# Reordering VectorE and ScalarE work at the end of the branch stage and in the output stage of a two-layer trunk kernel

## The reference, cut to what matters

```
proj = jnp.einsum('btnw,nwd->btnd', branches, p['w_branch'])        # four branches, each 256 wide
gsig = jax.nn.sigmoid(gates...)                                      # one gate per branch and channel
merged = jnp.sum(gsig * proj, axis=2)
x = x + g1 * (merged @ p['w_out'])
h2 = _rms(x, p['g_norm2']) * (1 + sc2) + sh2                         # needs the sum of squares of all of x
x = x + g2 * _conv_ffn(h2, p['w_up'], p['conv_w'], p['conv_b'], p['w_down'])
```

## Time and profile before

| | before |
|---|---|
| median of 3 executions | 1292.45 us |
| lowest and highest | 1290.4 and 1293.11 us |
| the profiled execution's own time | 1288.97 us |
| its span | 1287.2 us |
| PE busy | 1266.9 us, 98% |
| DVE busy | 787.5 us, 61% |
| ACT busy | 594.0 us, 46% |
| POOL busy | 85.8 us, 7% |
| mean granted TensorE clock | 1.00 |

### The profile page before, as it was taken

How to read it: one execution, slowest core, us unless ns; L and a number is a source line. 1 busy time by engine, 2 the same in 40 slices (tenths; PEclk the granted TensorE clock), 3 DMA queues, 4 the chain that set the end, 5 groups by cost and what they waited for, 6 DMA issues and landing times.

```text
span 1287.2 us, 20265 instructions
## 1 busy us (share of the span) xinstructions
PE 1266.9 (98%) x8210; PEld 1184.3 (92%) x8210; DVE 787.5 (61%) x1482; ACT 594.0 (46%) x989; POOL 85.8 (7%) x57
## 2 busy tenths in 40 slices
PE   7999999999999999999999999999999999999999
PEld 6987888889989999999989888888898899999998
DVE  5553286448778777763353543864496787778432
ACT  3456455543355445442344564645433654454321
POOL 0000000005410000000000000000082000000000
PEclk9999999999999999999999999999999999999999
DMA  9731344543633444448554313344336233333343
GB/s 374 287 131 57 118 172 147 197 148 111 232 135 130 158 153 154 154 158 280 175 214 142 115 66 115 115 159 147 120 130 241 90 130 131 123 123 131 131 134 129
DMA packets 52686, 198.11 MB, mean 154 GB/s; under 512 B 6320, under 2 KB 6736, under 8 KB 51184
## 3 DMA queue, kind: packets, MB, share of 16 engines
q1 hardware_dynamic: 52272, 196.11, 43.4%
q0 software_dynamic: 320, 0.69, 0.2%
HBM read 194.51 MB, written 2.26 MB: 153 GB/s over the span
## 4 chain that ended last, share of the span: by engine, by line
PE 88%; DVE 7%; ACT 1%; issue 1%; DMA 1%; SPq 0%; DVEq 0%
PE bank L1232 24%; PE bank L1234 24%; PE bank L1233 24%; PE bank L1191 2%; DVE w_lo L836 2%; PE bank L1482 1%; PE bank L1512 1%; PE bank L1492 1%; DVE merged_lo L1088 1%; DMA w_raw<-stream 1%; DVE gated_late L1103 1%; PE bank L1300 1%; PE bank L1301 1%; PE bank L1302 1%; DVE small L1051 1%
## 5 line engine op out<-in xcount | busy, mean ns | idle before, releaser
L1232 PE MATMUL bank<-act_hi,w_hi 128*128 128x384 f32 x1368 | 466.0, 341 | 1.1 <-DVE act_lo L880 0.7
L1234 PE MATMUL bank<-act_hi,w_lo 128*128 128x384 f32 x1368 | 457.8, 335 | 0.0
L1233 PE MATMUL bank<-act_lo,w_hi 128*128 128x384 f32 x1336 | 446.7, 334 | 0.0
L836 DVE TENSOR_TENSOR w_lo<-w_raw,w_hi 128x1024 fp32r<-128x1024 f32 x251 | 311.6, 1243 | 220.3 <-ACT w_hi L516 219.9
L516 ACT ACTIVATE w_hi<-w_raw 128x1024 fp32r<-128x1024 f32 x251 | 263.7, 1051 | 168.8 <-DMA w_raw<-stream 162.4
L1232 PEld LDWEIGHTS bank<-act_hi,w_hi 128*128 128x128 f32 x1368 | 257.3, 188 | 8.6 <-issue 5.1
L1234 PEld LDWEIGHTS bank<-act_hi,w_lo 128*128 128x128 f32 x1368 | 256.7, 188 | 0.0
L1233 PEld LDWEIGHTS bank<-act_lo,w_hi 128*128 128x128 f32 x1336 | 251.0, 188 | 0.9
L1232 PE MATMUL bank<-mlp_hi,w_hi 128*128 128x384 f32 x352 | 120.0, 341 | 0.0
L1233 PE MATMUL bank<-mlp_lo,w_hi 128*128 128x384 f32 x352 | 119.6, 340 | 0.0
L1234 PE MATMUL bank<-mlp_hi,w_lo 128*128 128x384 f32 x352 | 119.6, 340 | 0.0
(11 more groups left out here) (223 smaller groups left out, 1544.8 us busy)
## 6 DMA issues: line engine op xcount, KB each, us to landing
w_raw<-stream SPq DMA_DIRECT2D x251, 512.0 KB, 3.3
ada<-ada_w SPq DMA_DIRECT2D x56, 512.0 KB, 4.2
start_ada<-start_ada SPq DMA_DIRECT2D x8, 1024.0 KB, 17.5
ada_norm<-ada_w SPq DMA_DIRECT2D x16, 512.0 KB, 5.7
ada_head_a<-ada_w SPq DMA_DIRECT2D x8, 512.0 KB, 5.2
time_consts<-time_consts SPq DMA_DIRECT2D x2, 1920.0 KB, 9.3
start_raw<-start_w SPq DMA_DIRECT2D x8, 448.0 KB, 18.2
params<-params SPq DMA_DIRECT2D x2, 926.0 KB, 13.0
```

Source lines behind the costliest of these rows:

```text
L836: V.tensor_tensor(wlo[s][:, :], raw[s][:, :], whi[s][:, :].bitcast(F32), ALU.subtract).then_inc(lo_ready, 1)
L1232: T.matmul(out, wb[s][0][:, w, :], hi[k], start=first and k == 0, stop=False)
L1233: T.matmul(out, wb[s][0][:, w, :], lo[k], start=False, stop=False)
L1234: ins = T.matmul(out, wb[s][1][:, w, :], hi[k], start=False, stop=last and k == n - 1)
```

## The change

It moves instructions on DVE and ACT and adds or removes none. It applies to both layers.

- Branch stage, DVE: `merged_low(4)`, which stood between the split of O0+1 and the gatings of d = 7, is moved behind the split of O0+2. The order at the end is now: split O0, split O0+1, four gatings of d = 7, split O0+2, `merged_low` 4, 5, 6, 7.
- Output stage, DVE: `split(P0+2)`, which stood ahead of `residual(7)`, is moved behind it.
- Output stage, ACT: `square(0)` stands ahead of the split of O0+5 (before: O0+6), `square(2)` ahead of O0+7 (before: P0), `square(4)` ahead of P0+1 (before: P0+2). The split of P0+2 is moved behind the table load and the square of block 6, and ahead of the square of block 7. The residuals for which the squares wait are the same.

```
--- before.py
+++ after.py
@@ -746,16 +746,18 @@
                     if d >= 1:
                         act.wait_ge(merged_ready, l * KD + d)
                         A(mhi[:, d - 1, :], msum[:, (d - 1) % 4, :], ACT.Copy, scale=0.5).then_inc(mrg_hi, 1)
-                for d in range(KD):
-                    if d in (3, 5, 7):
-
-                        act.wait_ge(x1_ready, FROM + l * KD + d - 1)
-                        square(d - 3)
+                for d in range(KD - 1):
+                    if d in (2, 4, 6):
+
+                        act.wait_ge(x1_ready, FROM + l * KD + d)
+                        square(d - 2)
                     split(O0 + d + 3)
                 logs()
-                for k in (KD - 2, KD - 1):
-                    act.wait_ge(x1_ready, FROM + l * KD + k + 1)
-                    square(k, 1)
+                act.wait_ge(x1_ready, FROM + l * KD + KD - 1)
+                square(KD - 2, 1)
+                split(P0 + 2)
+                act.wait_ge(x1_ready, FROM + l * KD + KD)
+                square(KD - 1, 1)
                 norm(1)
                 tanhs()
 
@@ -1107,10 +1109,10 @@
                         split(B0 + d + 2)
                         if d == KD - 2:
                             split(O0 + 1)
-                        if d >= 2:
+                        if 2 <= d < KD - 2:
                             merged_low(d - 2)
                 split(O0 + 2)
-                for d in range(KD - 3, KD):
+                for d in range(KD - 4, KD):
                     merged_low(d)
 
                 def residual(d, b, gate0, done):
@@ -1120,12 +1122,14 @@
                     ins.then_inc(done, 1)
 
                 for d in range(KD):
-                    split(O0 + d + 3)
+                    if d < KD - 1:
+                        split(O0 + d + 3)
                     dve.wait_ge(unit_done, FROM + l * UNITS + O0 + d + 1)
                     residual(d, OUT_BANK[d % 4], 16, x1_ready)
                     if d == 0:
                         modulation(l, 4)
                         scales(sc2, 32, "g2")
+                split(P0 + 2)
                 norm(1)
                 modulation(l, 5)
```

## The result

| | before | after |
|---|---|---|
| median, four executions each | 1291.43 us | 1281.18 us |
| lowest and highest | 1289.75 and 1293.11 us | 1279.52 and 1281.63 us |
| ratio, 95% interval | | 0.9928 (0.991 to 0.9946) |
| profiled execution, its span | 1288.97 us, 1287.2 us | 1281.63 us, 1279.8 us |
| mean granted TensorE clock of the profiled execution | 1.00 | 1.00 |

The change is faster by 0.7%, 10.2 us between the medians. The direction was right; the gain was under-estimated.

The account below looks back on a forecast made before the run. PE, busy 98% of the span, bounds the kernel, leaving 20.3 us idle. 4.24 + 3.63 = 7.9 us off 1288.97 gives 1281.1, times 1.0027 makes 1284.6 us; range 1282.3 to 1289.5.

Parts of the forecast that it names:

- the stage sums: Branch stage 4.24 us plus output stage 3.63 us, over both layers: 7.9 us off the profiled execution.
- the output group's stall: End of the branch stage: PE stops at k = 2 for the split of O0+2; resumes 2.12 us earlier per layer.
- 2.12 + 1.84: Layer 0: 2.12 us from the branch stage, 1.84 us from line 1266 starting earlier at the output stage's end.
- The main case: End of the branch stage: split of O0+2 goes before POOL's add, 2.12 us gained per layer; chance 0.46.
- the tie: Branch stage, layer 0: split of O0+2 and POOL's line 509 add for d = 6 both start at 329.84 us.
- its rival: End of the branch stage: POOL's add goes first, 1.25 us gained per layer, 1286.3 us in all; chance 0.28.
- The thin covers: `merged_low(5)` hidden by 0.2 us, split of O0+5 by 0.35; up to 0.4 us a layer lost if both fail.
- `square(4)` was costed at nothing: Output stage, ACT: moved ahead of the split of P0+1, it waits for `residual(5)` alone; cost 0.
- 1.79 us: Output stage, layer 1: line 1266 could start at 1001.07 and not at 1002.86 us, a gain of this size.
- PE's wait of 0.41 us at O0+4 in layer 1: PE already waits this long for the load of O0+4; nothing counted for DMA.
- 1.0027: Final step: median of the runs over the profiled execution, turning 1281.1 into 1284.6 us.
- the two stalls: PE's two equal waits behind a `w_lo` split, branch stage of both layers, 4.5 us; removal counted as 4.24 us.

Follow-up runs that it names:

- tie_pool: Changed kernel plus one one-column VectorE instruction between the last gating and the split of O0+2, so POOL's line 509 add comes first: 1282.37 us, ratio 0.9942 to the kernel before.

## Why the prediction was wrong where it was, and right where it was

**Right: the stage sums.** From POOL's first add on, the two profiled executions can be laid over each other. The forecast for the end of the output group's stall was 2.12 us, measured 2.12 in layer 0 and 2.13 in layer 1. The up units start 4.09 us earlier in layer 0 (forecast 2.12 + 1.84 = 3.96). From there to the end of the span it is 984.93 against 976.94 us, 8.0 us for a forecast of 7.9. The main case, the split first at the tie, is the one that occurred, and `tie_pool` shows its rival with its price. The thin covers held: PE waits neither for the low rests nor for the split of O0+5.

**Right in sum by luck in layer 1: two errors that cancel.** `square(4)` was costed at nothing since POOL's sum would be ready. It was not, by 0.6 us, because the split of P0+1 and POOL's add met: gained 1.3 and not 1.79 us. On the other side, PE's wait of 0.41 us at O0+4 in layer 1, which I had left in place, did not occur in the changed kernel, nor in the second profile of the kernel before; so it is no property of the kernel.

**Wrong: the step from the profiled execution to the median.** The prediction summed to 1281.1 us for an execution like the profiled one and then multiplied by 1.0027, since the median of the kernel before lies 3.5 us above its profiled execution, and so came to 1284.6. That treats the 3.5 us as a property of every kernel. The runs show what it is made of, by the 84 executions of the table, whose median is 1290.2 us:

- 2.2 us is chance: the median of the three first executions, 1292.45, lay that far above 1290.2.
- 2.3 us is the distance from 1290.2 to the 1287.9 of the executions without a drop of TensorE's clock. The profiled execution had no drop; the median one has one or two.
- Less 1.1 us, by which the profiled execution, 1288.97, lay above 1287.9.

The drops come behind the very stalls that the change removes, and the changed kernel hardly has them: nine of its ten executions with a clock on record are at 1.000. So the term that was missing in the sum is the clock behind the two stalls, which I had priced at their length alone. Filling the wait put 2.4 to 2.8 us on it, of which up to 0.9 us may be something else. The range failed by the same step: its lower end allowed for scatter around 1284.6 and not for the scatter itself going.

That the sum without the factor, 1281.1, meets the measured 1281.18 so closely is luck in part. It starts from an execution 1.1 us above the others of its kind, and the gain between executions without a drop is 6.9 us (1287.9 and 1281.0), 1.0 less than the 7.9 of the sum; the two cancel.

The clue was in the times before: the profiled execution lay 1.4 us under the lowest of the three others (1288.97 and 1290.4), so it might be a special one, and a profile at 1.00 says nothing of the executions that were not profiled. I took the clock of one execution as that of the kernel.

**What stays open.** The stage gains of the profiles (8.0) and the difference between drop-free executions (1287.9 and 1281.0, 6.9 us) are 1.1 us apart. The wait of 0.41 us in the first profile may be part of it. Another part may be the opening of the program, which no edit touches: POOL's first add starts anywhere from 300.92 to 302.86 us in the twelve profiles (302.27 and 301.06 in the two of the kernel before, 302.86 and 302.85 in those of the changed one). That is 2 us of scatter without any of these stalls, and its cause was not traced. In the kernel before a drop does not always follow the wait (none in the first profile, behind both in the second), and what decides it was not looked for.

## What to carry to other kernels

A stall of PE can cost more than its length: price it with the drop of the clock behind it, at both levels, even if the one profile at hand shows a clock of 1.00; a profiled execution that is faster than all the others is the sign to look at more of them first. Before removing a stall, one can fill it with matmuls on constants: that tells how much of its price is the clock and not the wait. Where DVE instructions with two SBUF inputs and POOL's adds follow each other closely, write down who starts first at each meeting, since a lead of 0.01 to 0.07 us decided about 1 us behind.

## What the runs showed of the hardware that I had not expected

Behind a wait of 2.25 us on PE, between stretches in which it worked without a gap, the granted clock went from 1.00 to 0.50 (2.4 to 1.2 GHz) for about 3.4 us, and in the same kernel the same wait passed without a drop in another execution. With 7 matmuls in the wait (14 records, 1.72 us) the profile shows no drop behind it in either layer. The Trainium skill (TensorE: Matmul & The Clock Gate, Part 1) says that the slow level is the default and that activity releases it; the trace agrees in both directions: the clock fell behind the standstill and came back while PE was multiplying.
